# Banks and filling steps around the dilated attention of a fused two-block kernel

## What is computed

```python
qa, ka, va, qd, kd, vd, ga, gb = split(rmsnorm(x) @ w_in)
oa = diff_attention(rope(qa), rope(ka), va, lam)      # 8 heads, two softmaxes each, q in blocks of 128
for gi, (win, dil) in enumerate(((128, 1), (512, 4), (2048, 16))):
    o_g, lse_g = dilated_window_attention(rope(qd)[gi], rope(kd)[gi], vd[gi], dil, win // (2 * dil))
od = sum(softmax(lses) * outs)                        # 12 heads folded to 4 x 64 columns
merged = sigmoid(ga) * (oa @ w_proj_a) + sigmoid(gb) * (od @ w_proj_b)
x = x + rmsnorm(merged @ w_out)
```

## Time and profile before

| | |
|---|---|
| median of 3 runs | 2444.9 us |
| lowest, highest | 2443.22, 2446.3 us |
| the profiled execution's own time | 2446.42 us |
| its span | 2444.6 us |
| TensorE busy | 2388.4 us, 98% |
| VectorE, ScalarE, GpSimd busy | 51%, 39%, 8% |
| mean granted TensorE clock | 0.992 |
| differential scores (L1963) | 446.1 to 625.8 us |
| dilated scores (L1971) | 675.9 to 797.0 us |

### The profile page before, as it was taken

One profiled execution on the slowest core, in us unless ns is written; L12 is line 12 of the kernel. 1 busy time (PEld: TensorE's weight loads), 2 busy tenths in 40 slices (PEclk: granted clock), 3 DMA queues, 4 the chain that ended last, 5 costly groups with the idle time before them and its releaser, 6 DMA issues.

```text
span 2444.6 us, 28442 instructions
## 1 busy us (share of the span) xinstructions
PE 2388.4 (98%) x11206; PEld 1910.0 (78%) x11206; DVE 1235.2 (51%) x2012; ACT 963.1 (39%) x1613; POOL 196.1 (8%) x147
## 2 busy tenths in 40 slices
PE   8999999999999999999999999999999899999998
PEld 7888888777777778888887677888887677888887
DVE  5533436788654445433336855424435775532432
ACT  4323224465432334322324554313324784431432
POOL 0100100322102000100100200000001100000000
PEclk9999999999999999999999999999999999999999
DMA  4323323211222232323323113322222112333332
GB/s 147 104 86 102 98 91 103 74 52 52 70 69 72 63 108 79 103 80 110 95 81 99 61 53 100 108 95 95 95 93 67 30 45 80 99 100 95 95 95 70
DMA packets 66805, 208.50 MB, mean 85 GB/s; under 512 B 7408, under 2 KB 15856, under 8 KB 66416
## 3 DMA queue, kind: packets, MB, share of 16 engines
q1 hardware_dynamic: 66672, 206.68, 27.1%
HBM read 204.55 MB, written 2.10 MB: 85 GB/s over the span
## 4 chain that ended last, share of the span: by engine, by line
PE 90%; DVE 4%; ACT 3%; issue 2%; DMA 1%; POOL 0%; POOLq 0%; SPq 0%; DVEq 0%; ACTq 0%
PE bank L1834 26%; PE bank L1838 26%; PE bank L1836 26%; PE bank L2001 2%; PE bank L1963 1%; PE bank L2008 1%; DMA wraw<-in_stream 1%; PE bank L2054 1%; PE bank L1992 1%; PE bank L1909 1%; PE bank L1905 1%; DVE wlo L2427 1%; PE bank L1907 1%; ACT whi L2122 1%; PE bank L1928 1%
## 5 line engine op out<-in xcount | busy, mean ns | idle before, releaser
L2427 DVE TENSOR_TENSOR wlo<-wraw,whi 128x1024 fp32r<-128x1024 f32 (+5 forms) x436 | 489.3, 1125 | 541.1 <-ACT whi L2122 538.0
L1834 PE MATMUL bank<-hhi,whi 128*128 128x512 f32 x1736 | 690.6, 398 | 10.2 <-ACT whi L2122 8.1
L1838 PE MATMUL bank<-hhi,wlo 128*128 128x512 f32 x1736 | 679.0, 391 | 1.1 <-DVE wlo L2427 1.1
L1836 PE MATMUL bank<-hlo,whi 128*128 128x512 f32 x1736 | 678.1, 391 | 0.7 <-DVE hlo L2434 0.7
L2122 ACT ACTIVATE whi<-wraw 128x1024 fp32r<-128x1024 f32 (+5 forms) x436 | 409.5, 942 | 488.4 <-PE bank L1838 423.0
L1834 PEld LDWEIGHTS bank<-hhi,whi 128*128 128x128 f32 x1736 | 326.9, 188 | 82.4 <-ACT whi L2122 9.8
L1838 PEld LDWEIGHTS bank<-hhi,wlo 128*128 128x128 f32 x1736 | 326.3, 188 | 73.3 <-DVE wlo L2427 3.6
L1836 PEld LDWEIGHTS bank<-hlo,whi 128*128 128x128 f32 x1736 | 327.1, 188 | 67.3 <-DVE hlo L2434 2.8
L1836 PE MATMUL bank<-mlo,whi 128*128 128x512 f32 x576 | 227.6, 395 | 0.2 <-DVE mlo L2734 0.2
L1834 PE MATMUL bank<-mhi,whi 128*128 128x512 f32 x576 | 227.6, 395 | 0.0
L1838 PE MATMUL bank<-mhi,wlo 128*128 128x512 f32 x576 | 227.5, 395 | 0.0
(11 more groups left out here) (417 smaller groups left out, 3098.9 us busy)
## 6 DMA issues: line engine op xcount, KB each, us to landing
wraw<-in_stream SPq DMA_DIRECT2D x343, 512.0 KB, 3.5
wraw<-in_stream SPq DMA_DIRECT2D x32, 192.0 KB, 2.4
wraw<-in_stream SPq DMA_DIRECT2D x22, 256.0 KB, 2.6
wraw<-in_stream SPq DMA_DIRECT2D x26, 128.0 KB, 2.0
wraw<-in_stream SPq DMA_DIRECT2D x8, 320.0 KB, 2.9
xa<-in_x SPq DMA_DIRECT2D x8, 256.0 KB, 6.2
out<-ya SPq DMA_DIRECT2D x8, 256.0 KB, 2.7
m<-in_mask SPq DMA_DIRECT2D x1, 1024.0 KB, 4.9
```

Of the source, the lines that this page charges most:

```text
L1834: pe.matmul(out, sh, xh, start=first, stop=False)
L1836: pe.matmul(out, sh, xl, start=False, stop=False)
L1838: p = pe.matmul(out, sl, xh, start=False, stop=end and last)
L2427: dve.tensor_tensor(wlo[j][:, 0:L], wraw[i][:, 0:L], whi[j][:, 0:L].bitcast(f32), SUB).then_inc(*lo.up(c))
```

## The change

```diff
@@ -730,7 +730,7 @@
             yield from qk_tile(("qd", 2 * g, 0))
             yield from qk_tile(("kd", 2 * g, 0))
 
-    share_banks(2)
+    G.slots, SB.slots = bank[4:6], bank[0:4]
     filler["gen"] = stream_diff()
     fill(12)
     heads = {}
@@ -845,9 +845,10 @@
 
     filler["gen"] = stream_dil()
     last, owed = None, 0.0
+    fill(2)
     first, second = ([dil_unit(p, i) for i in range(4)] for p in range(2))
     for unit in first + [None] + second + [None]:
-        pace = 1 if unit else 5
+        pace = 5 if not unit else 1 if last else 1.5
         for l, fills in ((unit, 1.1), (last, 1), (last, 1), (last, 0), (unit, 1), (last, 0), (unit, 0)):
             if l:
                 next(l, None)
```

## The result

The changed kernel takes **2451.5 us** in the median of 9 runs (2449.3 to 2455.0). The kernel before, run beside it, takes 2446.3 us, also in 9 runs. The ratio is 1.0024, with a 95% interval of 1.0016 to 1.0033, so the change costs about 5 us (4 to 8 by the interval). The profiled execution took 2450.21 us, with a span of 2448.4. Forecast was 2453.0, in a range of 2446.5 to 2457.0.

What follows compares the result with a forecast made beforehand. TensorE, busy 98% of the span, was taken as the bound. Terms -1.15, 0, -1.15, +0.94, +5.9, -0.7 gave +3.8; clock +4.3 made +8.1 us on 2446.4, less 1.5 for the median: 2453.0, range 2446.5 to 2457.0.

Steps and rivals of the forecast that it cites:

- Banks of the differential stage: Head of the differential stage: first product takes bank 5, free earlier, instead of bank 1; gain 1.15 us, bounds 0 and 1.2.
- Two calls ahead of the scores: Before the first dilated scores: the first call waits where the scores waited; 0 us, bounds -0.3 and +0.2.
- the ring's parity: Before the first dilated scores: odd bank index makes the calls open bank 1, still being copied, passing the wait on.
- First dilated turn: First turn of the dilated stage: a 12-matmul call covers more of PE's wait on soft; gain 1.15 us, bounds 0 and 1.7.
- Calls without a matmul between turns: Units (0,2) and (1,0): matmul-free filling calls fall between turns 1 and 2, exposing one more place net; +0.94 us.
- The tail: Last dilated units: filling matmuls run out after turn 1 of (1,1), exposing the chains; loss 5.9 us, bounds 4.4 and 7.5.
- Sum at a full clock: Whole kernel: all terms, including -0.7 us for calls directly behind each other, without a clock fall; +3.8 us.
- The clock: Tail and products behind: thin PE use lowers the granted clock to 1.2 GHz; +4.3 us, bounds 0 and +8.
- Rival 3: Tail: the clock falls already after turn 2 of (1,1), through both units; +3.8 and 8, 2456.7 us; chance 0.12.
- Rival 1: Tail: the clock stays at 2.4 GHz; +3.8 us, 2448.7 us; chance 0.17.
- Rival 2: Tail: covered after all because soft of (1,2) and (1,3) comes early; not slower, 2442.9 us; chance 0.09.
- Rival 4: Before the first dilated scores: the two calls don't remove the wait; within the forecast, 1.2 us less if it went.

Runs made afterwards that it cites:

- e1: The kernel before with only the new banks in the differential stage; ratio to the kernel before 1.0003, touched stretch 393.78 us against 394.90.
- e4: The changed kernel with other banks in the dilated stage, free long before the two calls ahead open them; ratio to the kernel before 1.0024.
- e9: The changed kernel plus three unused matmuls behind each dilated turn from turn 2 of (1,1), seven behind the output of (1,2); ratio to the kernel before 1.0017.
- e3: The changed kernel with pace 1.5 only in round 0's first unit and round 0's None step at pace 4; ratio to the kernel before 0.9997.
- e7: The changed kernel plus five unused matmuls behind each dilated turn from turn 2 of (1,1), ten behind the output of (1,2); ratio to the kernel before 1.0018.
- e2: The changed kernel with the old bank sharing back in the differential stage, so the filling change alone; ratio to the kernel before 1.0038.
- e6: The kernel before with only pace 1.5 in the first unit of each round, no calls ahead; ratio to the kernel before 1.0017.
- e5: The kernel before with only two filling calls ahead of the first dilated scores, at the old pace; ratio to the kernel before 1.0014.

## Why the prediction was right, and which term was not

**Banks of the differential stage**: -1.15 forecast, 1.39 to 0.23 measured, -1.16. e1 shows it alone. Right, and kept, as argued.

**Two calls ahead of the scores**: 0 forecast. The wait was passed on to the first call as the ring's parity said (1.06 us on L2589 at 674.99). From the last vd product to the next start it is 1.34 for 1.52 before, a gain of 0.18 inside the bounds. e4 shows that the bank decides.

**First dilated turn**: idle from 1.67 to 0.55 forecast, 0.36 measured (a little under the 0.4 to 0.7 that was to show it). Soft took 3.29 us beside GpSimd's rope, as assumed. Timeline of DVE and of POOL in the kernel after:

```profile
689.31 3.29 DVE L2662 TENSOR_SCALAR eb<-eb,sm 128x768 f32<-128x768 f32 x2
...
807.80 1.15 DVE L2662 TENSOR_SCALAR eb<-eb,sm 128x768 f32<-128x768 f32 x2
```
```profile
689.31 1.29 POOL L2912 TENSOR_TENSOR ftmps<-ftmps,rs 128x512 f32<-128x512 f32 x1 [1.88 <-DVE ftmps L2604]
690.67 1.50 POOL L2918 TENSOR_TENSOR qk<-ftmps 128x512 f32<-128x512 f32 x1
```

With GpSimd quiet the same soft takes 1.15. The Trainium skill (SBUF — State Buffer, "SBUF: two separate sides") has the port pair that VectorE and GpSimd share as an exclusive lock and not a split of bandwidth. The trace agrees in kind, with soft 2.1 us longer beside 2.8 us of GpSimd work. It doesn't show which port an instruction used.

**Calls without a matmul between turns**: two for one, +0.94 forecast. They are the waits at 722.28 and 787.52, in the units (0,2) and (1,0) that were named; the one at 778.11 is gone.

**The tail**: here the forecast can be laid beside the timeline row by row. From turn 2 of (1,1) at 803.15, forecast 1.29, 2.64, 4.10, 5.83, 9.88, 13.07 and 17.12 (the last output, 1.35 behind the last turn), measured 1.29, 2.64, 4.10, 5.85, 9.88, 13.09 and 17.12. Loss 5.9 at a full clock, as in e9 (803.28 to 821.88, 18.6 us). This was the term that decided, and e3, without it, is 6.9 us shorter than the changed kernel (the 1.5 of the clock among it).

**Sum at a full clock**: +3.8 forecast. e9 measures +3.82. So close an agreement is partly luck. The scores and the first turn each gained 0.2 us more than forecast, and the differential stage 0.1 (210.84 for 210.94); the places without a matmul and the calls directly behind each other, which no run takes apart, must have cost about 0.4 us more than booked.

**The clock** is the term that was mis-sized: "Taken together +4.3, if the clock falls before (1,3)'s turns", measured 1.5. The fall was right, and so was its cause, as far as two executions can show it (e7 and e9 kept the clock in the same chain). Its place was not. In the profiled execution the turns of (1,3) still stood 1.35 apart (1.2 us forecast, 0 measured), the output gave 1.2 (1.4 forecast), and the products behind were slow for two starts, 0.4 us (1.7 forecast). That last part had been taken from the odd mixer, where the low clock lay over nine starts. How much dense work the low clock covers depends on where it fell, so the price of that stretch could not be carried over without its place. e2, e4 and e6 show the fall before the last two turns, with a share of about 2.4 us, so the term also varies between executions of nearly the same tail. Rival 3's fall (already after turn 2 of (1,1)) was seen in none of the three executions with the whole tail (after, e2, e4).

The forecast of +8.1 was thus 2.8 too high in the trace, all of it clock, and 2.9 too high in the timed difference of 5.2. That 2453.0 came only 1.5 above the median measured is luck: the kernel before, which it was counted from at 2444.9, had a median of 2446.3 in the nine runs beside the changed one. Rival 1 (+3.8) has the right sum without the clock; it fails on the 0.80 of the window 818 to 822. Rival 2, a tail that is covered after all, fails on the rows above: exp behind the third copy, soft late by 1.69 us. Rival 4 is half true: the wait was passed on.

What stays open is what decides where the clock falls, and whether it does. In the tail it was at 1.00 in all three executions with a tail of 5.5 us (before, e1, e3), and fell in all five with one of 10 us or more. But the odd mixer was not "the only like place of the trace", as the prediction has it. Windows of the kernel before, in a later stage that no kernel here changes (its longest gap of PE up to the fall is 0.66 us):

```profile
1402.00:1407.00 5.00, 3.31 (x24) 1.70 (x22) 4.39 (x18) 3.75 (x11) 0.00 (x0) 1.00 0.00 0
1407.00:1414.00 7.00, 5.57 (x31) 3.92 (x32) 5.36 (x19) 4.36 (x12) 2.54 (x2) 0.53 0.01 2
```

And the same place in e3:

```profile
1403.00:1410.00 7.00, 3.72 (x29) 2.35 (x31) 5.61 (x19) 5.59 (x15) 2.55 (x2) 1.00 0.01 2
```

Here the clock fell behind 5 us of thin use, shorter than the old tail. The same steps kept their clock in the profiled executions of e3 and e5 and lost it in the other eleven. So the length of a thin stretch doesn't decide by itself, and one execution of a kernel doesn't settle what the clock does in the next.

## What to carry to other kernels

Moving calls of filling forward covered one wait of 1.7 us and left five more turns and outputs bare at the end, so count the calls through to the last unit before judging the gain at the first, and read the price of a bare place from the spacing of starts (0.94 us), not from the idle column (0.69). A call should be no larger than the gap that it covers (6 matmuls and not 12, here), and the step that frees a bank must be issued ahead of anything in its queue that waits for later work. A chain that can't be covered may still lower the clock of what follows; matmuls of no use that fit in its waits kept it at 1.00 here.

## What the runs showed that was not expected

- The granted clock fell to 1.2 GHz in stretches where no single gap of PE was over 1.7 us (816.24 in the kernel after, 1.69). With three matmuls of 128x128 in each gap behind a turn and seven in the long one it stayed at 2.4 GHz (e9, one execution), at no cost to the chain.
- The same chain loses the clock at different places. e6's turns slowed from 816.7 on, the changed kernel's only behind 820.27, although its tail had been thin for longer; 0.9 us of e6's and e2's loss is that alone.
- After the fall the clock was back within 1 us of dense products in the changed kernel (two slow starts, 822.94 and 823.54), while the earlier trace rows has it low over 3.8 us of them.
